# Two blocks of a hybrid network: the hyena projection, the recurrent projection and the gate projections computed from seven quarter products instead of eight

## The reference

```python
# first block: h is the normed, modulated x
q, k, v, g, hy_u, gate_ret, gate_hy = split(h @ w_in + b_in)       # hy_u: 1536 columns, the gates: 2 x 1024
x0, x1, v = split(short_conv(hy_u, conv_w, conv_b), 3)              # taps over tokens t-1, t, t+1
mixed = sigmoid(gate_ret) * (ret_gated @ ret_w_o) + sigmoid(gate_hy) * (hy_out @ hy_w_o)
x = x + gt1 * (mixed @ w_out)                                       # then a mixture of 32 experts
# second block
z = h @ w_in                                                        # z_rwkv: 1920 columns, z_gate: 2 x 1024
zf = z + mu_prev * (z_prev - z) + mu_next * (z_next - z)            # shift over tokens, all 1920 columns
kk = heads(k * k_k); kk = kk / max(sqrt(sum(kk * kk)), 1e-12)       # k: 4 of the 15 column tiles
s = qn . k_nope + qr . k_rope; p = softmax(s * scale); o = p @ v    # 8 heads, query blocks of 128
mixed = sigmoid(gates0) * (o_mla @ w_br_mla) + sigmoid(gates1) * (o_rwkv @ w_br_rwkv)
```

## Time and profile before

| | us |
|---|---|
| median of 3 runs (4590.42 to 4597.82) | 4591.13 |
| the profiled execution | 4586.46 |
| its span, first to last instruction | 4584.3 |
| TensorE matmul busy | 4100.4 (89%) |
| DVE / ACT / POOL busy | 1280.9 / 1016.0 / 455.3 |

### The profile page before, as it was taken

One profiled execution on the slowest core, in us unless ns is written; L12 is line 12 of the kernel. 1 busy time (PEld: TensorE's weight loads), 2 busy tenths in 40 slices (PEclk: granted clock), 3 DMA queues, 4 the chain that ended last, 5 costly groups with the idle time before them and its releaser, 6 DMA issues. The chain is left out here.

```text
span 4584.3 us, 95914 instructions
## 1 busy us (share of the span) xinstructions
PE 4100.4 (89%) x41717; PEld 2659.3 (58%) x41717; DVE 1280.9 (28%) x2323; ACT 1016.0 (22%) x2426; POOL 455.3 (10%) x655
## 2 busy tenths in 40 slices
PE   7898799998999969999978897979999989997995
PEld 2343345885444458888853443459889844444774
DVE  2424321132000220000043553235666521012002
ACT  2200110022000112222243331024444300011433
POOL 1010000000000000000010000024545400000112
PEclk8899899999999979999989999989999999998998
DMA  5361211103111179999950001100000031113998
GB/s 210 120 184 64 93 56 64 37 10 103 33 32 30 58 267 393 397 392 394 398 183 10 8 2 42 37 5 4 4 4 4 4 122 48 32 59 138 389 390 318
DMA packets 246296, 588.57 MB, mean 128 GB/s; under 512 B 36264, under 2 KB 153943, under 8 KB 226360
## 3 DMA queue, kind: packets, MB, share of 16 engines
q1 hardware_dynamic: 203087, 454.52, 27.2%
q0 software_dynamic: 26976, 103.32, 6.7%
q10 hardware_dynamic: 16010, 27.46, 1.7%
HBM read 514.20 MB, written 71.05 MB: 128 GB/s over the span
## 5 line engine op out<-in xcount | busy, mean ns | idle before, releaser
L1544 PE MATMUL experts_bank<-experts_uT,ex_wu 128*64 128x96 f32 x9216 | 390.6, 247 | 26.6 <-PE experts_bank L1530 22.2
L1544 PEld LDWEIGHTS experts_bank<-experts_uT,ex_wu 128*64 128x64 f32 x9216 | 384.1, 138 | 43.5 <-issue 43.5
L192 PE MATMUL vgproj_bank<-vg_w,mix_hT 128*128 128x256 f32 x1024 | 225.5, 383 | 11.1 <-DVEq L201 7.6
L1176 DVE TENSOR_TENSOR merge_pr<-merge_bank,merge_sg 128x512 f32<-128x512 f32 x64 | 44.3, 692 | 681.6 <-ACT merge_sg L1163 408.0
L1617 DVE TENSOR_TENSOR experts_hT<-experts_si,experts_bank 128x384 f32<-128x384 f32 (+1 forms) x68 | 31.3, 460 | 722.3 <-PE experts_bank L1544 722.3
L1734 PE MATMUL taps_bank<-b2z_hT,taps_w 128*128 128x512 f32 x480 | 211.5, 599 | 21.6 <-DMA taps_w<-in_w_in 15.5
L1149 PE MATMUL merge_bank<-mix_hT,merge_w 128*128 128x512 f32 x512 | 222.3, 592 | 0.0
L1149 PE MATMUL merge_bank<-b2z_hT,merge_w 128*128 128x512 f32 x512 | 222.3, 592 | 0.0
L192 PEld LDWEIGHTS vgproj_bank<-vg_w,mix_hT 128*128 128x128 f32 x1024 | 195.6, 192 | 41.4 <-DVEq L201 8.5
L1544 PE MATMUL experts_bank<-experts_uT,b2z_hT 128*64 128x96 f32 x4096 | 177.9, 248 | 25.7 <-DMA b2z_hT<-in_w 15.3
L1544 PEld LDWEIGHTS experts_bank<-experts_uT,b2z_hT 128*64 128x64 f32 x4096 | 172.4, 138 | 40.3 <-issue 40.3
(11 more groups left out here) (501 smaller groups left out, 6497.4 us busy)
## 6 DMA issues: line engine op xcount, KB each, us to landing
ex_wu<-in_expert_w SPq DMA_DIRECT2D x72, 2048.0 KB, 17.4
mixed_T<-in_expert_w SPq DMA_DIRECT2D x36, 2048.0 KB, 19.8
b2z_hT<-in_w SPq DMA_DIRECT2D x64, 1024.0 KB
b2z_Z<-in_w SPq DMA_DIRECT2D x32, 1024.0 KB, 12.7
keep_rows<-mix_hyT POOLq DMA_DIRECT2D x27, 768.0 KB, 4.7
keep_rows<-experts_yo ACTq DMA_DIRECT2D x68, 288.0 KB
mix_hT<-in_ada_w POOLq DMA_DIRECT2D x8, 2048.0 KB, 10.3
merge_w<-in_w_in SPq DMA_DIRECT2D x32, 512.0 KB, 5.8
```

Source lines behind the costliest of these rows:

```text
L192: last = pe.matmul(bk[t][:, 0:width], xT[:, k, t * P:(t + 1) * P], wt[:, s, k, :], start=(k == 0), stop=(k == KT - 1))
L1176: dve.tensor_tensor(pr[:, h, j, :], bk[4 * h + 2 + j][:, :], sg[:, h, j, :], ALU.mult).then_inc(prod, 1)
L1544: last = pe.matmul(bk[2 + j][c:c + 64, h * BT:(h + 1) * BT], wu[:, s, j, k, h * P + c:h * P + c + 64], uT[:, s, k, :], start=(k == 0), sto ...
```

## The change

A product of a 2x2 grid of blocks, weights (two column tiles or two channel halves) by tokens, is computed from seven block products and a few sums instead of eight block products. The left blocks are weights with 4 x 128 channels each, the right blocks quarters of `hT` (4 channel groups, 512 tokens). A block product is 4 matmuls in one PSUM bank.

- In the hyena's and the recurrent projection two column tiles make a pair, with 28 matmuls instead of 32 (class `Pairs`). DVE makes four sums of token quarters once, into `K.X`; POOL makes the sums of weights for each pair; ACT copies the first product out, DVE folds the seven products into the four results, taps follow. Weights come 1 MB a pair. There is no loop any more. The fifteenth recurrent tile is made alone.
- In the merges the grid is (two gates) by (two channel halves) of one column tile, so each tile loses 4 matmuls; the branch products go first, in the order 2, 3; the sigmoid is now taken of the folded sum in SBUF. `K.X` holds the token sums, so its four parts and a small table are loaded at the end, behind the last tile's product M5; the others of POOL's transfers go ahead.
- The clears of "hin" are issued by ACT, five behind each pair.
- `phase_rwkv_consts`, "taps" and `phase_rwkv_gates` become one stage, `phase_rwkv_inputs`: tables are loaded beside the pairs, the squares of k and their small matmuls stand behind the pairs 3 to 6.
- In the attention heads the two value tiles of an even step and the odd step behind it are made at the odd step.

```diff
+def quarters(x):
+    return [[x[:, k * 4:k * 4 + 4, h * HALF:(h + 1) * HALF] for h in range(2)] for k in range(2)]
+        turn = (2, 3, 0, 1)
+        (b11, b12), (b21, b22) = quarters(hT)
+        t1, t2, t3 = [slab[:, 2 * n:2 * n + 2, :].rearrange("p a (b n) -> p (a b) n", b=2) for n in range(3)]
+        t4 = b12
+        part = lambda s, n: w[:, s, 4 * n:4 * n + 4, :]
+        A0, B0, B1, A1, M1, M6, M7, M5, M2, M4, M3, STEP = range(1, 13)
...
+                    sp.wait_ge(mm, i * (2 * STEP) + (s * STEP - STEP))
...
+            sp.wait_ge(mm, 7 * STEP + M5)
+            for to, what in late:
+                sp.dma_start(to, what, allow_slow_non_contiguous=True).then_inc(lated, 16)
+            sp.wait_ge(lated, 16 * len(late))
...
+            for to, what in ahead:
+                gp.dma_start(to, what, allow_slow_non_contiguous=True).then_inc(asided, 16)
...
+                    then(gp.tensor_tensor(s1, a21, a22, ALU.add))
+                    then(gp.tensor_tensor(s2, s1, a11, ALU.subtract))
+                    gp.tensor_tensor(a21, a11, a21, ALU.subtract)
+                    gp.tensor_tensor(s4, a12, s2, ALU.subtract).then_inc(sums, 1)
...
+                    for n, (j, h) in enumerate(((2, 0), (3, 0), (3, 1), (2, 1))):
...
+                        if j == 3 and h == 0 and ahead:
+                            pe.wait_ge(asided, 16 * len(ahead))
+                        pe.wait_ge(prod, i * 8 + (4 * s + (2, 3, 1, 4)[n]))
...
+                    for j in range(2):
+                        pe.wait_ge(full[s][j], i * 16 + 16)
+                    if came is not None:
+                        pe.wait_ge(came[0], 16 * came[1])
+                    pe.wait_ge(sig, i * 8 + (4 * s + 4))
+                    for k in range(4):
+                        last = pe.matmul(bk[0][:, :], w[:, s, k, :], b11[:, k, :], start=(k == 0), stop=(k == 3))
+                    last.then_inc(mm, 1)
...
+                    act.wait_ge(summed, i * 4 + (2 * s + 1))
+                    hold(act, mm, i * (2 * STEP) + (s * STEP + M1))
+                    act.activation(sg[:, 0, 0, :], bk[0][:, :], ACT.Identity).then_inc(copied, 1)
...
+                    dve.wait_ge(copied, i * 2 + (s + 1))
+                    dve.wait_ge(mm, at_step(M6))
+                    dve.tensor_tensor(u[:, 0, :], bk[1][:, :], sg[:, 0, 0, :], ALU.add).then_inc(folded, 1)
...
+                    dve.wait_ge(mm, at_step(M5))
+                    dve.tensor_tensor(sg[:, 1, 1, :], bk[3][:, :], u[:, 1, :], ALU.add).then_inc(ready, 1)
+                    dve.tensor_tensor(u[:, 0, :], bk[3][:, :], u[:, 0, :], ALU.add).then_inc(folded, 1)
+                    dve.wait_ge(mm, at_step(M2))
+                    dve.tensor_tensor(sg[:, 0, 0, :], bk[0][:, :], sg[:, 0, 0, :], ALU.add).then_inc(ready, 1)
+                    times(s, 1, 3, 1)
+                    dve.wait_ge(mm, at_step(M4))
+                    dve.tensor_tensor(sg[:, 1, 0, :], bk[2][:, :], u[:, 1, :], ALU.add).then_inc(ready, 1)
+                    times(s, 2, 2, 0)
+                    dve.wait_ge(folded, at_fold(3))
+                    dve.wait_ge(mm, at_step(M3))
+                    dve.tensor_tensor(sg[:, 0, 1, :], bk[3][:, :], u[:, 0, :], ALU.add).then_inc(ready, 1)
+                    times(s, 3, 3, 0)
+                    total(s, 0, 3)
+                    times(s, 4, 2, 1)
+                    total(s, 1, 4)
...
+class Pairs:
+    M1, M2, M4, M6, M7, M5, M3 = range(1, 8)
...
+    def request(self, sp, w, p):
+        if p >= 2:
+            sp.wait_ge(self.mm, 7 * (p - 1))
+        sp.dma_start(self.w[:, p % 2, :, :, :].rearrange("p k n c -> p k (n c)"), w[:, :, 2 * p * P:2 * (p + 1) * P]).then_inc(self.full[p % 2], 16)
+    def token_sums(self, dve):
+        dve.tensor_tensor(self.t1, self.b12, self.b11, ALU.subtract).then_inc(self.made, 1)
+        dve.wait_ge(self.made, 1)
+        dve.tensor_tensor(self.t2, self.b22, self.t1, ALU.subtract).then_inc(self.made, 1)
+        dve.tensor_tensor(self.t3, self.b22, self.b12, ALU.subtract).then_inc(self.made, 1)
+        dve.wait_ge(self.made, 2)
+        dve.tensor_tensor(self.t4, self.b21, self.t2, ALU.subtract).then_inc(self.made, 1)
+    def weight_sums(self, gp, p):
+        (a11, a21), (a12, a22) = [[self.w[:, p % 2, 4 * k:4 * k + 4, n, :] for n in range(2)] for k in range(2)]
+        s1, s2, s4 = [self.ws[:, n, :, :] for n in range(3)]
+        gp.wait_ge(self.full[p % 2], 16 * (p // 2) + 16)
+        if p:
+            gp.wait_ge(self.mm, 7 * p)
+        gp.tensor_tensor(s1, a21, a22, ALU.add).then_inc(self.added, 1)
+        gp.wait_ge(self.added, 2 * p + 1)
+        gp.tensor_tensor(s2, s1, a11, ALU.subtract).then_inc(self.added, 1)
+        gp.wait_ge(self.added, 2 * p + 2)
+        gp.tensor_tensor(a21, a11, a21, ALU.subtract)
+        gp.tensor_tensor(s4, a12, s2, ALU.subtract).then_inc(self.sums, 1)
+    def products(self, pe, p):
+        def quarter(bank, left, right):
+            for k in range(4):
+                last = pe.matmul(self.bk[bank][:, :], left(k), right[:, k, :], start=(k == 0), stop=(k == 3))
+            last.then_inc(self.mm, 1)
+        raw = lambda half, n: (lambda k: self.w[:, p % 2, 4 * half + k, n, :])
+        summed = lambda n: (lambda k: self.ws[:, n, k, :])
+        pe.wait_ge(self.full[p % 2], 16 * (p // 2) + 16)
+        if p:
+            pe.wait_ge(self.copied, p)
+        quarter(0, raw(0, 0), self.b11)
+        if p:
+            pe.wait_ge(self.folded, 7 * p - 6)
+        quarter(1, raw(1, 0), self.b21)
+        pe.wait_ge(self.made, 4)
+        if p:
+            pe.wait_ge(self.folded, 7 * p - 1)
+        quarter(2, raw(1, 1), self.t4)
+        pe.wait_ge(self.sums, p + 1)
+        quarter(3, summed(1), self.t2)
+        quarter(4, raw(0, 1), self.t3)
+        quarter(5, summed(0), self.t1)
+        if p:
+            pe.wait_ge(self.folded, 7 * p)
+        quarter(6, summed(2), self.b22)
+    def copy(self, act, p):
+        if p:
+            act.wait_ge(self.folded, 7 * p - 5)
+        act.wait_ge(self.mm, 7 * p + self.M1)
+        act.activation(self.u[:, 0, :], self.bk[0][:, :], ACT.Identity).then_inc(self.copied, 1)
+    def fold(self, dve, p, out, bias=None):
+        bk, u = self.bk, self.u
+        def add(bank, x, o, n=None):
+            if bias is None or n is None:
+                ins = dve.tensor_tensor(o, bk[bank][:, :], x, ALU.add)
+            else:
+                ins = dve.scalar_tensor_tensor(o, bk[bank][:, :], bias(2 * p + n), x, ALU.add, ALU.add)
+            ins.then_inc(self.folded, 1)
+        dve.wait_ge(self.copied, p + 1)
+        dve.wait_ge(self.mm, 7 * p + self.M2)
+        add(1, u[:, 0, :], out(0, 0), 0)
+        dve.wait_ge(self.mm, 7 * p + self.M6)
+        add(3, u[:, 0, :], u[:, 1, :])
+        dve.wait_ge(self.folded, 7 * p + 2)
+        dve.wait_ge(self.mm, 7 * p + self.M7)
+        add(4, u[:, 1, :], u[:, 2, :])
+        dve.wait_ge(self.folded, 7 * p + 3)
+        dve.wait_ge(self.mm, 7 * p + self.M5)
+        add(5, u[:, 2, :], out(1, 1), 1)
+        add(5, u[:, 1, :], u[:, 1, :])
+        add(2, u[:, 2, :], out(1, 0), 1)
+        dve.wait_ge(self.folded, 7 * p + 5)
+        dve.wait_ge(self.mm, 7 * p + self.M3)
+        add(6, u[:, 1, :], out(0, 1), 0)
+        dve.wait_ge(self.folded, 7 * p + 7)
...
+                pairs.copy(act, p)
+                for to, what in aside[p * each:(p + 1) * each]:
+                    act.dma_start(to, what).then_inc(asided, 16)
+            act.wait_ge(asided, 16 * len(aside))
...
+                pairs.fold(dve, p, lambda n, h: up[:, n, 1 + h * HALF:1 + (h + 1) * HALF], bias)
+                for n in range(2):
+                    t = 2 * p + n
+                    o = zc[:, t, :]
+                    then(dve.tensor_scalar(o, up[:, n, 0:SEQ], tap(0, t), tap(3, t), ALU.mult, ALU.add))
+                    then(dve.scalar_tensor_tensor(o, up[:, n, 1:SEQ + 1], tap(1, t), o, ALU.mult, ALU.add))
+                    dve.scalar_tensor_tensor(o, up[:, n, 2:SEQ + 2], tap(2, t), o, ALU.mult, ALU.add)
...
+                if p == 1:
+                    for to, what in tables:
+                        sp.dma_start(to, what).then_inc(came, 16)
+            sp.wait_ge(pairs.mm, 7 * (NPAIRS - 1))
+            sp.dma_start(odd, w[:, :, LAST * P:(LAST + 1) * P]).then_inc(pairs.full[NPAIRS % 2], 16)
...
+                if p == 3:
+                    pe.wait_ge(came, 16 * len(tables))
+                for q in range(max(p - 3, 0), max(p - 2, 0)):
+                    for h in range(2):
+                        pe.wait_ge(squared, 2 * q + h + 1)
...
+                        last.then_inc(normed, 1)
+            pe.wait_ge(pairs.full[NPAIRS % 2], 16 * (NPAIRS // 2) + 16)
...
+            for h in range(2):
+                act.wait_ge(single, h + 1)
+                act.activation(up[:, 0, 1 + h * HALF:1 + (h + 1) * HALF], bk[h][:, :], ACT.Identity).then_inc(evac, 1)
+            act.wait_ge(conv, LAST + 1)
```

(50 more changed lines are left out.)

311 lines of the change are left out of this document (172 added, 139 removed).

## The result

The changed kernel takes 4420.61 us (median of 4 runs, 4412.71 to 4424.4) against 4590.77 for the kernel before beside it: ratio 0.9627, 95% interval 0.9606 to 0.9649. That is 170 us faster where 150 were forecast (4441, range 4415 to 4475). The profiled execution took 4423.86, 162.6 less than the profiled one of before.

A forecast was written before the change was run, and what follows sets the result against it. TensorE's matmul count sets the touched stages' time, with start and tail around it. Gains 24.3 + 42.3 + 28.0 + 28.0 + 32.6 = 155.2 us, less 5, give 4436.3 profiled, 4441 as median; range 4415 to 4475.

The forecast's parts named there:

- the late tiles of X: At each merge's end, X transfers and small table tie with the last sum: counted as nothing, bounds 0 and 9 us.
- the allowance of 5: Over the whole kernel, 5 us taken off the summed gain for small waits of the pairs.
- Hyena projection: In the hyena projection, 168 matmuls replace 192; stage 160.7 us against 185.0, a gain of 24.3 us.
- Recurrent inputs: Constants, recurrent projection and norms as one stage: 210.2 us against 252.5, a gain of 42.3 us.
- Merges: Each merge loses 32 matmuls: 376.0 and 321.0 us against 404 and 349, a gain of 28.0 us each.
- The loop turns: In each merge the loop is kept and its three turns cost 0.9 us each, 2.7 us.
- nothing again, at most 5: In the first merge, the first hyT matmul's wait for hyT and the scattered write costs nothing, at most 5 us.
- Heads: In the attention heads, six value-bank waits and the lower clock behind them go: a gain of 32.6 us.
- The 1 us taken off for the key copy: In the attention heads, 1 us less gain because the key copy ahead of an even head loses a little cover.
- POOL, 3 of allowance: At the 11 changes of pair, POOL's weight sums cost 0.3 us each if engines take turns; bounds 0 and 23 us.
- the rival in which POOL loses to all six shifts: At 11 changes of pair TensorE waits 2 us for POOL's weight sums; 4460 us, chance 0.12.
- Rival (c): At each of 11 pair changes, POOL's chain makes TensorE wait 13.6 us or more: 4591 us and up, chance 0.03.

The follow-up runs named there:

- the longer chain: The changed kernel with four more POOL additions ahead of each pair's weight sums in both projections: 4488.45 us, ratio 0.9777 against the kernel before.

## Why the prediction was right, step by step

The mechanisms held. The count of matmuls set the four stages, the heads' six waits went but for 0.53 us at one change, POOL kept ahead, the late tiles of X tied with the last sum (the small table landed about 1 us ahead of it: issued at 1420.78, 10.6 us, last sum to 1432.5). It was 20 us low on the gain by the medians and 12 by the profiled executions (4436.3 for 4423.86). That is 14 by the five stages (155.2 for 169.0) and the allowance of 5 that nothing needed, less the 6 that the untouched stages took more in that execution. Its terms:

- **Hyena projection, 160.7 for 162.2.** Start 6.9 (said 6.0), low clock 3.0 (1.6), matmuls 144.3 (144.5), tail 8.0 (8.6). The first two quarter products took 9.98 for 7.03, so the low clock cost 3.0 here and not 1.6; in the other three stages it was 1.8 to 2.5.
- **Recurrent inputs, 210.2 for 201.8.** The mis-sized term: 32 small matmuls at the price of the lower clock, 13.8, where the four groups took 6.8. The price was read from a row of the stage that had lost its clock. Start 5.4 (6.3) and tail 5.4 (6.2) gave another 1.7.
- **Merges, 376.0 for 378.0 and 321.0 for 314.2.** Three misses. The start was taken over from the earlier trace rows though what slowed it, POOL's transfer, leaves with the change (or, in the first merge, comes 0.3 us later behind the slab): the starts of 4.25 and 4.6 were 4.6 and 4.4 shorter than said, shown above. The loop turns cost nothing (2.7 said): before, their 0.9 was the wait for a DVE product, and the branch products that now open a step need one that is long there. In the timeline the last block of a step (1157.52, 3.60 us) and the first behind the turn (1160.95) stand without a gap. And the first merge's scattered write was priced at "nothing again, at most 5": it took 18.5 and not 9, and cost 9.3 with the clock, of which 5.8 came back without it. In the first merge this cancelled the other two, so that 376.0 lies near 378.0 is luck; the second merge, without such a write, shows them.
- **Heads, 32.6 for 35.0,** and 36 when undone. The 1 us taken off for the key copy is there as 0.8: TensorE's waits for it grow from 5.1 to 5.9 us.
- **POOL, 3 of allowance for 0.** Said: 10.1 us if the engines take turns, with four of DVE's instructions between the additions; measured 7.35. The starts and ends above fit turns instruction by instruction: POOL's second addition starts as DVE's first shift is under way and ends 1.1 behind it, the next shift ends 1.1 behind that, and so on; three instructions get in, one to a gap, and I had allowed four. I had also priced them at 4.7 us together; the three lengthen POOL's additions by 0.3, 0.9 and 1.0, 2.2 in all. The Trainium skill ("SBUF — State Buffer", section "SBUF: two separate sides") calls the shared pair "an exclusive lock, not a bandwidth split", held for the whole instruction. The trace agrees: POOL's first addition of the stage, beside a token sum of 2.28 us that began 0.11 earlier, takes 3.29 and the later ones 1.26. What the rule was read for, the rival in which POOL loses to all six shifts, was wrong, and to call it the plain reading was too: the section says how long the pair is held, and holding the lock for an instruction isn't holding it for a sequence.
- **Rival (c), slower from a wait of 13.6 us at each change,** left out the clock: the waits with the longer chain carried 2.3 us of it a change, and that of 6.1 in the first merge 3.1. The measured gain of 170 is 15.5 us a change, so waits of 12 to 13 us each would do (an estimate, which takes the clock's share behind such a wait to be 2.3 to 3.1 as well; no run has one).

What stays open: why the branch slab of 256 KB took 13.9 us in the first merge even with the gate weights held back (asked for at 1056.12, TensorE released at 1070.00; hyT landed and the gate weights were asked for at 1065.3, and the scattered write was under way until 1073.7); why that write takes 14 to 18.5 us at a stage's start, when nothing that shared the engines with it was taken away alone; and what the written-out code costs or gives, since no kernel with loops around the pairs was run.

## What to carry to other kernels

Price an operation from a row in the clock state that it will have after the change, and read a stage's start for what shares the transfer engines with it: a duration taken over from before carries the company it had. When a wait counts several transfers, name the slowest of them by its landing time; a scattered 8 KB write can be later than 2 MB. For a helper engine in series with TensorE, work out the slack (here 10.1 against 7.35) and remember that past it the waits bring the lower clock with them (here half their length again).

## What the runs showed of the hardware

- A row of 64 records of small matmuls (moving size 2) lost the granted clock while TensorE was busy throughout: 1.00 in the first 1.7 us, 0.50 from 3.7 us on, even right behind 24 large ones. In the groups of 16 (1.7 us) between large matmuls it stayed.
- A scattered 8 KB write took 18.5 us behind a 2 MB transfer, and 14.0 ahead of it, and the 2 MB then landed after 19.5 instead of 10.6. Why it is slow is open.
- DVE and POOL, each with back-to-back instructions on SBUF, took turns instruction by instruction: those of 1.27 and 1.28 us (two inputs) are shown as 2.1 to 2.3, and DVE's shift with one input, 0.81 alone, as 1.08 and 1.75.
- At the merges' starts TensorE has its first slab (512 KB, or 256 KB and two of 128) 3.9 to 4.6 us behind the request when POOL asks for nothing or asks 0.45 us later, and after 8.5 to 8.9 with 1 or 2 MB asked for 0.1 us behind it; SyncE's next slab follows 0.4 to 0.6 us behind the first in all of them.
